# Delta stage of a hybrid streaming encoder: one turned update per level issued later, an inverse root and a state sum issued earlier

## The reference

```python
m = jnp.where(strict, jnp.einsum('bhnid,bhnjd->bhnij', kb, k) * decay, 0.0)
a = m + jnp.eye(L, dtype=f32)
sol = lax.linalg.triangular_solve(a, rhs, left_side=True, lower=True, unit_diagonal=True)
attn = jnp.einsum('bhnid,bhnjd->bhnij', q, k) * decay

def step(st, inp):
    qd, kcd, wv, at, kt, gt = inp
    v_new = wv - jnp.einsum('bhld,bhde->bhle', kcd, st)
    o = jnp.einsum('bhld,bhde->bhle', qd, st) + jnp.einsum('bhij,bhje->bhie', at, v_new)
    st = st * gt[..., None, None] + jnp.einsum('bhld,bhle->bhde', kt, v_new)
    return st, o
```

## Time and profile before

| | |
|---|---|
| median of 3 runs | 2990.32 us (2989.4 to 2992.2) |
| the profiled execution's own time | 2988.97 us |
| its span, first to last instruction | 2987.2 us |
| mean granted clock of TensorE | 0.990 |
| busy shares of the span | PE 97%, PEld 93%, DVE 62%, ACT 28%, POOL 49% |
| pairs 1 to 7 of the delta stage | 35.8 to 37.7 us each, 256.0 us in all |

### The profile page before, as it was taken

One profiled execution on the slowest core, in us unless ns is written; L12 is line 12 of the kernel. 1 busy time (PEld: TensorE's weight loads), 2 busy tenths in 40 slices (PEclk: granted clock), 3 DMA queues, 4 the chain that ended last, 5 costly groups with the idle time before them and its releaser, 6 DMA issues. The chain is left out here.

```text
span 2987.2 us, 55758 instructions
## 1 busy us (share of the span) xinstructions
PE 2888.0 (97%) x23320; PEld 2763.4 (93%) x23320; DVE 1866.9 (62%) x3041; ACT 836.8 (28%) x1560; POOL 1455.9 (49%) x1026
## 2 busy tenths in 40 slices
PE   8999999999999999999999979999999999999998
PEld 7999767999999999998999968888899999999998
DVE  2337675685656576677775636666487656557666
ACT  2212475233232321012321223333133323231011
POOL 2233101347676752225832217887546777763224
PEclk9999999999999999999999989999999999999999
DMA  6120102022222242212332234332413222224222
GB/s 181 45 59 16 50 2 89 8 81 69 76 77 76 78 167 100 88 45 89 115 97 88 75 96 108 89 89 59 135 36 89 73 80 73 80 83 160 88 81 75
DMA packets 278416, 243.82 MB, mean 82 GB/s; under 512 B 51305, under 2 KB 251351, under 8 KB 277655
## 3 DMA queue, kind: packets, MB, share of 16 engines
q1 hardware_dynamic: 278167, 240.26, 26.2%
HBM read 177.32 MB, written 62.91 MB: 80 GB/s over the span
## 5 line engine op out<-in xcount | busy, mean ns | idle before, releaser
L160 PE MATMUL ps<-xhi,whi 128*128 128x364 f32 x2352 | 780.6, 332 | 9.4 <-PEq L922 3.6
L161 PE MATMUL ps<-xlo,whi 128*128 128x364 f32 x2352 | 774.1, 329 | 0.0
L166 PE MATMUL ps<-xhi,wlo 128*128 128x364 f32 x2352 | 773.2, 329 | 0.0
L160 PEld LDWEIGHTS ps<-xhi,whi 128*128 128x128 f32 x2352 | 441.2, 188 | 15.1 <-issue 8.9
L161 PEld LDWEIGHTS ps<-xlo,whi 128*128 128x128 f32 x2352 | 441.6, 188 | 3.0
L166 PEld LDWEIGHTS ps<-xhi,wlo 128*128 128x128 f32 x2352 | 441.1, 188 | 1.4
L1599 POOL TENSOR_SCALAR whi<-wraw 128x1024 fp32r<-128x1024 f32 x88 | 111.0, 1262 | 578.6 <-PE ps L166 526.5
L1873 PE MATMUL ps<-xhi,wlo 128*128 128x272 f32 (+1 forms) x1216 | 352.2, 290 | 0.0
L1872 PE MATMUL ps<-xlo,whi 128*128 128x272 f32 (+1 forms) x1216 | 352.1, 290 | 0.0
L1871 PE MATMUL ps<-xhi,whi 128*128 128x272 f32 (+1 forms) x1216 | 351.0, 289 | 0.0
L2384 DVE TENSOR_TENSOR z<-ps,z 128x364 f32<-128x364 f32 x384 | 202.8, 535 | 144.7 <-PE ps L166 144.7
(11 more groups left out here) (513 smaller groups left out, 6696.8 us busy)
## 6 DMA issues: line engine op xcount, KB each, us to landing
wraw<-in_w_ff_in SPq DMA_DIRECT2D x88, 512.0 KB, 4.6
wraw<-in_w_ff_out SPq DMA_DIRECT2D x44, 512.0 KB, 4.1
qkvz<-eo_ob SPq DMA_DIRECT2D x32, 546.0 KB, 4.6
wraw<-in_w_in_o SPq DMA_DIRECT2D x32, 512.0 KB, 4.4
xlo<-hidden SPq DMA_DIRECT2D x28, 546.0 KB, 5.3
hidden<-eo_ups SPq DMA_DIRECT2D x18, 546.0 KB, 2.7
hidden<-oo_ups SPq DMA_DIRECT2D x18, 546.0 KB, 2.8
z<-residual SPq DMA_DIRECT2D x6, 1456.0 KB, 9.4
```

What stands on the lines that cost most here:

```text
L160: one = pe.matmul(out, whi, xhi, start=start, stop=False)
L161: two = pe.matmul(out, whi, xlo, start=False, stop=False)
L166: return pe.matmul(out, wlo, xhi, start=False, stop=stop)
```

## The change

Three parts, all in `delta_block`, with no arithmetic changed:

1. Levels 2 to 5 of the pairs with two chunks (`skewed`): the turned update of half 1 is issued after the cross product of half 0 of the next level, and that of level 5 at the end. T has a semaphore of its own (YT, counted by the update), so VectorE subtracts from T without waiting for the turned update of the same half. The products move to other PSUM banks: cross products and updates of half 0 to bank 4 and of half 1 to bank 6, turned updates to banks 5 and 7 (bank 1 for half 0 of the last level, which waits for oln).
2. ScalarE: the exponential that makes rk goes ahead of the copy of the values.
3. VectorE: `state_add` of chunk 0 goes ahead of the mask product of L3403.

```diff
+        def cross_at(A, l, b):
+            return bank1(b if l == 1 else (4, 6)[b] if A.nb == 2 else 4)
+        def update_at(A, l, b):
+            return bank1((4, 6)[b] if skewed(A, l) else 6 + b)[:, 0:GR]
+        def turned_at(A, l, b):
+            if skewed(A, l):
+                return bank1((1 if l == LEVELS - 1 else 5, 7)[b])[:, 0:GR]
+            return bank1(6 + b)[:, GR:H]
...
+                        cross(A, l, 0)
+                        if skewed(A, l - 1):
+                            turned_update(A, l - 1, 1)
+                        if A.nb == 2:
+                            cross(A, l, 1)
...
                         for b in range(A.nb):
...
+                                update(A, l, b)
+                            if b == 0 or not skewed(A, l):
+                                turned_update(A, l, b)
                         if B and l == 2:
                             squares_sum(B)
+                    if A.nb == 2:
+                        turned_update(A, LEVELS - 1, 1)
...
+                    act.wait_ge(s("kln"), A.th(1, 1))
+                    act.activation(rk[:, 0:A.J, :], rk[:, 0:A.J, :], ACT.Exp, scale=-0.5).then_inc(s("rk"), 1)
                     act.wait_ge(s("vturned"), A.th(1, 1))
...
                     act.copy(vt[A.odd][:, 0:A.J, :], bank2(6)[:, 0:A.J, :]).then_inc(s("vt"), 1)
-                    act.wait_ge(s("kln"), A.th(1, 1))
-                    act.activation(rk[:, 0:A.J, :], rk[:, 0:A.J, :], ACT.Exp, scale=-0.5).then_inc(s("rk"), 1)
...
+                if B:
+                    state_add(B, 0)
+                if A:
                     dve.wait_ge(s("TTa"), A.th(1, 1))
...
                     dve.tensor_tensor(bank1(6)[:, 0:J], bank1(6)[:, 0:J], low[:, 0:J], ALU.mult).then_inc(s("Ta"), 1)
-                if B:
-                    state_add(B, 0)
-                if A:
...
+                            if skewed(A, l) and l < LEVELS - 1:
+                                dve.wait_ge(s("YT"), A.th(A.group(l - 2, b), 2 * (LEVELS - 3)))
+                            else:
+                                dve.wait_ge(s("Y"), A.th(A.group(l - 1, b), 2 * (LEVELS - 1)))
```

More of the change, by code:

```diff
@@ L2820, in bank2, with skewed @@
             return m.ps[:, b:b + 2, :].rearrange("p b (h c) -> p (b h) c", c=P)[:, :, 0:n]
+        def skewed(A, l):
+            return A.nb == 2 and l >= 2
+        def cross_at(A, l, b):
[6 more added lines that the diff above has]
+            return bank1(6 + b)[:, GR:H]
         def chunks(x, p):
@@ L3151, in turn, with cross, ready, update @@
                 ins.then_inc(s(name), 1)
+            def cross(A, l, b):
+                pe.wait_ge(s("T"), A.th(A.group(l - 1, b), 2 * (LEVELS - 1)))
+                settle(pe, s("settled_pe"))
+                for h, half, j in places(b):
+                    ins = pe.matmul(cross_at(A, l, b)[half, j, :], ML[half, l - 1, j, :], T[half, j, :],
+                                    start=True, stop=True)
+                ins.then_inc(s("X"), 1)
+            def ready(A, l, b):
+                pe.wait_ge(s("TT"), A.th(A.group(l - 1, b), 2 * LEVELS))
+                pe.wait_ge(s("Xs"), A.th(A.group(l - 1, b), 2 * (LEVELS - 1)))
+            def update(A, l, b):
+                ready(A, l, b)
+                settle(pe, s("settled_pe"))
+                for h, half, j in places(b):
+                    ins = pe.matmul(update_at(A, l, b)[half, j - GR * b, :], solved(A)[half, j, :], X[half, j, :],
+                                    start=True, stop=True)
+                if skewed(A, l):
+                    ins.then_inc(s("YT"), 1)
+            def turned_update(A, l, b):
+                ready(A, l, b)
+                if l == LEVELS - 1 and b == 0 and A.nb == 2 and not A.first:
+                    pe.wait_ge(s("oln"), A.th(0, 1))
+                settle(pe, s("settled_pe"))
+                for h, half, j in places(b):
+                    ins = pe.matmul(turned_at(A, l, b)[half, j - GR * b, :], X[half, j, :], solved(A)[half, j, :],
+                                    start=True, stop=True)
+                ins.then_inc(s("Y"), 1)
             def run(A, B, C):
@@ L3218, in run @@
                         for b in range(A.nb):
-                            pe.wait_ge(s("TT"), A.th(A.group(l - 1, b), 2 * LEVELS))
-                            pe.wait_ge(s("Xs"), A.th(A.group(l - 1, b), 2 * (LEVELS - 1)))
-                            settle(pe, s("settled_pe"))
                             if l < LEVELS - 1:
[L3223 to L3229, removed]
+                                update(A, l, b)
+                            if b == 0 or not skewed(A, l):
+                                turned_update(A, l, b)
                         if B and l == 2:
                             squares_sum(B)
+                    if A.nb == 2:
+                        turned_update(A, LEVELS - 1, 1)
                 elif B:
@@ L3312, in run @@
                             act.wait_ge(s("X"), A.th(A.group(l - 1, b), 2 * (LEVELS - 1)))
-                            act.copy(X[:, hs, :], bank1(X_BANK[l] + b)[:, hs, :]).then_inc(s("Xs"), 1)
+                            act.copy(X[:, hs, :], cross_at(A, l, b)[:, hs, :]).then_inc(s("Xs"), 1)
                         if B and l == 1:
```

10 lines of the change are left out of this document (5 added, 5 removed).

## The result

The changed kernel took 2995.88 us in the median of 20 runs, one of which was disturbed (6663.9 us); the other 19 lie between 2993.03 and 2998.39, with a median of 2995.58. The kernel before took 2991.97 us (2988.77 to 2994.9, 20 runs). The ratio is 1.0015, 95% interval 1.0009 to 1.0021: some 4 us slower by the medians, where 8.5 us less were forecast.

A forecast was written before the change was run, and what follows sets the result against it. TensorE's idle time inside the delta stage was taken to bound the kernel. Terms 0.8 + 3.0 + 5.8 - 1.1 = 8.5 us gave a forecast median of 2981.8 us, range 2978.0 to 2986.5.

The forecast's parts named there:

- The inverse root: Keys' scaling ahead of gram_k: 0 in pairs 2 to 7, blocked by GpSimd's dn_Sg; 0.8 us gained in pair 0.
- the two cases: Pair 0's key scaling: up to 1.2 us gained if VectorE gets through first, 0 if GpSimd does.
- The state sum: Wait before old_values of chunk 1 goes: 0.43 us in each of pairs 1 to 7, 3.0 us in all.
- just fits: new_values of chunk 1 would be due at 1901.99, with VectorE's L3415 before it ending at 1901.97.
- The levels: Passages to levels 4 and 5 lose 0.36 us each, 5.8 us over eight pairs; level 3's passage costs 1.1 together.
- 5.0 - 1.1: Level terms for pairs 1 to 7: gain at passages to levels 4 and 5, less the loss at level 3's.
- the added waits: 24 more semaphore-wait rows on TensorE, decoded while it computes, at most some 0.02 us each: nothing to 0.5 us.
- The rival of the instruction supply: TensorE, waiting less, runs into cuts inside blocks because instructions come no faster: 3007.4 us, slower; chance 0.04.
- threshold: New cuts inside TensorE's blocks decide the outcome from about 1.7 us a pair (8.5 + 6 over 8).
- three cuts in eight pairs of like content: Argument against slow instruction supply: only pairs 2, 4 and 6 had a block cut, 1.33 us in pair 4.

The follow-up runs named there:

- rk_alone: Kernel before with only the exponential that makes rk put ahead of the copy of values on ScalarE: 2991.12 us, ratio 0.9999.
- sum_alone: Kernel before with only the state sum put ahead of the mask product on VectorE: 2987.2 us, ratio 0.9987.
- rk_and_sum: Kernel before with the ScalarE and VectorE parts of the change, the levels in their old order: 2986.81 us, ratio 0.9982.
- Skew_alone: Kernel before with only the turned update of half 1 put behind the next level's first cross product: 3002.03 us, ratio 1.0034.
- the padded kernels: 128 extra semaphore increments on TensorE ahead of the first stage, in the changed kernel (3010.5 us, ratio 1.0065) and the kernel before (3006.79 us, 1.0051).
- streak: Kernel before with the turned update of half 1 in the last level done 24 times more in each pair with two halves: 3086.67 us.
- the doses: Changed kernel with no, one or two semaphore increments ahead of each level product: 2982.59, 2995.88 and 3018.95 us.

## Why the prediction was wrong

*The inverse root.* Right: nothing in pairs 1 to 7 (rk_alone), with the scaling blocked to 1.08 us behind dn_Sg in every profile. In pair 0 VectorE got through first, and the keys end 1.2 us earlier, the upper bound, where I took 0.8 as a mean of the two cases. That the pair itself is 1.4 us shorter may be in part the clock: TensorE was at 1.2 GHz for 14.7 us of it before and for 11.1 in rk_alone.

*The state sum.* Right in kind, 3.0 forecast, 4.0 us measured in the profile of sum_alone. The term was read too small: I let `old_values` start 0.06 us behind the end of `gram_q`'s loads, but where nothing is awaited it starts 0.93 us after their start (1898.14 to 1899.07), ahead of their end. Before it was 1.50 (1896.80 to 1898.30), so 0.57 us go in each of seven pairs, not 0.43. `new_values` of chunk 1, of which I wrote that it "just fits", did not become the next wait.

*The levels.* The hand-overs did what was forecast: no idle time in levels 4 and 5, and 1.49 us at level 3. Between the profiles of the change and of rk_and_sum lie 10.7 us in pairs 1 to 7; cuts make 11.1 and the clock 3, so net of both the skew gave 3.5 us, of 5.0 - 1.1 = 3.9 forecast. Skew_alone against before says much the same: 11.7 us more, of which 11.7 are cuts, and 10.2 us at 1.2 GHz, up to 4.7 lost by the price above, so a gain of up to 4.7. Both rest on that price, taken from the level blocks, so this is an estimate.

*The step that failed* is the one that priced the added waits: "it has them decoded while it computes, except at most some 0.02 each: nothing to 0.5". I counted 24 rows, where the trace has 75 more records, and I overlooked the increment behind each wait. An increment takes TensorE 0.15 us to pass, as the padded kernels show; it is hidden from the blocks' pace and not from the instruction supply, and with the covering waits of 0.36 us gone it was paid as 12.4 us of cuts and 3 us of clock. How much of this is due to the 68 increments that the change adds, and how much to the 170 that were there and lost their cover, no run separates: none has the new order with the old number of increments. In proportion the 68 would make 12.4 x 68 / 238 = 3.5 us, an estimate.

*The rival of the instruction supply*, given 0.04, is what happened. Its threshold (about 1.7 us of new cuts a pair; the sum given for it, 8.5 + 6 over 8, makes 1.8) stood for a loss of 6 us; 12.4 over 7 is 1.8, and the loss was 4 us by the medians. Its 3007 us was too much, and its mechanism was half right: not instructions that "come no faster than now" (streak), but packets late behind waits and increments. The argument against it, "three cuts in eight pairs of like content", was poor: where a boundary falls changes with any edit, and the earlier trace rows showed 1.33 us that I could not explain.

The Trainium skill (Runtime: NRT & Kernel Launch, Instruction fetch mechanics) says that instructions come in blocks of 256, fetched while the current block executes, at a cost that is mostly hidden. The 256 agrees with the trace, and so does "hidden" in streak; in the skewed levels it is not hidden, up to 2.9 us at one boundary.

*Open:* what exactly asks for a packet. In the changed kernel's pairs 1, 4 and 6 the boundary before falls into level 2, ahead of level 3's wait, and the late packet begins 1.7 to 2.9 us after that wait is released. That TensorE's issue, slowed by increments and without a lead after a wait, asks late is argued from this and from the doses, not shown. I found no rule that gives the times of all packets.

## What to carry to other kernels

Count every instruction that a new order adds to an engine, bare semaphore increments too, and look how long one takes when several stand in a row. In streams of very short matmuls look for stops inside a block, at every 256th instruction: where they exist, waits removed elsewhere may come back there, and leaving out instructions can be worth more than reordering: here the 170 increments gave 4.9 us, the skew without increments nothing beyond that. When a wait is shortened, ask first whether the next engine's queue (here `differences` on VectorE) sets the same moment anyway.

## What the runs showed that I had not expected

- Semaphore increments in a row on TensorE follow each other every 0.15 us; 128 of them take 19.4 us.
- In all 17 traces the packets landed at each 256th record were as many as the places passed before it or one more: the supply was never more than one packet ahead.
- Leaving out the increments ahead of the level products, one each, gave the kernel before 4.9 us and the changed one 13.3 (medians 2991.55 to 2986.7, 2995.88 to 2982.59), with no work changed and only 67 and 74 records fewer.
- 256 instructions of TensorE in 3.73 us can be supplied without a stop; behind waits one boundary cost up to 2.9 us.
- Idle times of 0.82 and 2.10 us in pair 4 of the changed kernel, and of 1.44 and 1.99 in pair 6, were followed by 3.4 us at 1.2 GHz; 1.49 and 1.96 in pair 1 and 1.49 and 2.90 in pair 3 were not.
- A queue that is relieved in one place can hold the next: the clip moved out of level 3's way made level 4 wait 0.53 us.
